# A feed-forward weight block in eight gets its low part by an adding DMA

## The chip, the cores and the metric

The kernel runs on one NeuronCore of one Trainium2 chip. The metric is the device time of one execution in microseconds. A core has a matrix engine (TensorE, PE in the profile, with its weight loads as PEld), VectorE (DVE), ScalarE (ACT), GpSimd (POOL), and SyncE (SP), which here only issues DMAs. DMAs run on 16 DMA engines; those issued by SP are "hardware dynamic", those issued by GpSimd "software dynamic".

## The reference

Two transformer blocks follow each other on 256 tokens of width 2048, in fp32. The first has differential attention, a gated recurrence, cross attention and a feed-forward; the second a pooling mixer, gated linear attention and a feed-forward. The change touches only the two feed-forwards:

```python
FFN_HIDDEN = ((8 * D_MODEL // 3 + 255) // 256) * 256      # 5632
h = rms_norm(x, ffn_pre_g[l])
gate, up = jnp.split(h @ w_ffn_in[l], 2, axis=-1)
x = x + rms_norm((jax.nn.silu(gate) * up) @ w_ffn_out[l], ffn_post_g[l])
...
f = (jax.nn.silu(h @ w_ffn_gate[l]) * (h @ w_ffn_up[l])) @ w_ffn_down[l]
x = x + rms_norm_2(f, norm_ffn_post[l])
```

## The kernel before

All weights come as one stream of 961 slots of 128 x 1024 fp32 (512 KB). Every matrix product is made from two parts of each operand in the format fp32r: a high part, which is the value copied into fp32r, and a low part, which is value less high part. Three products (high x high, high x low, low x high) make up for the short mantissa.

A slot passes through four buffers of each kind (NR = NH = 4):

- SP (`sync`, L2339) loads slot i into `RAW[i % 4]`. It may do so when the low part of slot i-4 has been made, since that is the last to read RAW.
- ScalarE (`scalar`, `upto`, L1054) copies RAW into `RH[i % 4]`, when the load has landed and slot i-4 has been multiplied.
- VectorE (`vector`, `upto`, L1554) writes `RL[i % 4] = RAW - RH`. Six slots in the program have this done by GpSimd instead (`on_pool`, L2173); none of them is in the set that the change takes.
- TensorE (`tensor`) waits for the high part by `s_hi` and for the low part in `wait_low`, multiplies, and counts `s_slot`.

Every engine has its instructions in a fixed order. The order of copies and side work is set by `through`: for each slot i of a group, `upto(i + LA)` with LA = 3 makes the parts up to slot i+3, then the side tasks of slot i follow, and at the last slot of a pass the eviction of its results.

A gate or up group has 8 slots, two passes of four. `by_feature` multiplies a slot as 8 matmuls with the high weights (each 512 columns, high and low activations together) and 8 with the low weights (256 columns). At even positions of a pass the high ones come first, at odd positions (`turned`) the low ones. So TensorE's rows show runs of 16 high and 16 low matmuls: a low run holds positions 0 and 1 or positions 2 and 3, a high run positions 1 and 2 or position 3 and the next pass's 0. Four pairs of PSUM banks serve the passes in turn.

At the end of a pass ScalarE copies the low sum out of PSUM (128x512, L1039). VectorE adds the high sum and multiplies by the row scale. At the end of a gate group ScalarE then takes silu (128x1024, AR<-AR); at the end of an up group VectorE multiplies by the gate and ScalarE writes the high part of the hidden activations (B_HL<-AR in the first feed-forward, A_HL<-AR in the second). Only after these does ScalarE go on to the high copy of slot last+4, which is position 3 of the next group's first pass. The copies for positions 0 to 2 have been made before.

The first feed-forward ("F") has groups Fg0, Fu0, Fg1, ... in three parts (0 to 3, 4 to 7, 8 to 10), each followed by four output groups (Fo0_0 ...). The second ("H") has the same order. The first slot of Fg0 is 176, that of Fg1 192, and every F group starts at a multiple of 8. That of Hg0 is 697, and every gate or up group of H starts at a multiple of 8 plus 1.

Of the kernel before, what the change touches and what calls it, by code (L numbers as in the profile page):

```python
# [7 lines left out]
F32 = mybir.dt.float32  # L8
# [3 lines left out]
ALU = mybir.AluOpType  # L12
# [16 lines left out]
NR, NH, LA = 4, 4, 3  # L29
# [123 lines left out]
def build(nc, A, out, scratch):  # L153
    ctx = ExitStack()
    with ctx:

        def sb(name, shape, dt=F32):
            return ctx.enter_context(nc.sbuf_tensor(name, shape, dt))

        def sem(name):  # L160
            return ctx.enter_context(nc.semaphore(name))

        RAW = sb("RAW", [P, NR, 1024])
        RH = sb("RH", [P, NH, 1024], F32R)
        RL = sb("RL", [P, NH, 1024], F32R)
# [17 lines left out]
        def U(k, n=1):  # L183
            return AR[:, k * 2048:(k + n) * 2048]
# [25 lines left out]
        slots, passes, unit, turns = [], {}, {}, [0]  # L210
# [23 lines left out]
        groups = {n: [i for ids in passes[n] for i in ids] for n in passes}  # L234

        def first(name):
            return groups[name][0]
# [4 lines left out]
        def low_rank_parts(i):  # L242

            return [R[:, i % NH, :].rearrange("p (k r n) -> p k r n", r=4, n=32) for R in (RH, RL)]

        def low_rank_raw(i):
            raw = RAW[:, i % NR, 0:256].rearrange("p (k n) -> p k n", n=16)
            return [raw[:, 8 * h:8 * h + 8, :].unsqueeze(2).broadcast_to([P, 8, 4, 16]) for h in range(2)]  # L250
# [10 lines left out]
        on_pool = {i for n in ("cq", "co0", "co1", "Fg0", "Hg0") for i in groups[n][1:2]} | {first("K0")}  # L261
        pool_before = [sum(j in on_pool for j in range(i)) for i in range(len(slots) + 1)]


        s_eye, s_gains, s_load, s_memld = sem("eye_loaded"), sem("gains_loaded"), sem("setup_loaded"), sem("mem_loaded")
        s_x, s_xt, s_table = [sem(f"x_loaded_{q}") for q in range(4)], [sem(f"x_turned_loaded_{c}") for c in range(5)], sem("table_wanted")
# [2 lines left out]
        s_raw = [sem(f"raw_loaded_{r}") for r in range(NR)]  # L269
        s_first_raw, s_first_hi = sem("first_half_slot_loaded"), sem("first_half_slot_high_made")  # L270
        s_hi, s_lo_v, s_lo_p = sem("high_made"), sem("low_made_by_vector"), sem("low_made_by_pool")
        s_slot, s_half = sem("slot_multiplied"), sem("first_half_multiplied")
        s_init = sem("pool_constants_set")
        s_low_sum = sem("low_sum_copied")
# [151 lines left out]
        for x in range(4):  # L426
            j, part = x // 2, x % 2
# [92 lines left out]
        def tensor(g):  # L520
# [7 lines left out]
            def wait_low(i):  # L528
                if i in on_pool:
                    g.wait_ge(s_lo_p, pool_before[i + 1])  # L530
                else:
                    g.wait_ge(s_lo_v, i + 1 - pool_before[i + 1])

            def wait_unit(name, p=0):
                if name in norm_of and p == 0:
# [498 lines left out]
        def scalar(g):  # L1034
# [3 lines left out]
            def act(o, i, f=ACT.Copy, scale=1.0, bias=0.0, accum=None):  # L1038
                return g.activation(o, i, f, bias=bias, scale=scale, accum_out=accum)  # L1039

            def upto(n):
                while made[0] <= min(n, len(slots) - 1):
                    i = made[0]
                    made[0] += 1
                    g.wait_ge(s_raw[i % NR], 16 * (i // NR + 1))
                    if i >= NH:
                        g.wait_ge(s_slot, i - NH + 1)
                    if i == first("LR"):
                        for both, raw in zip(low_rank_parts(i), low_rank_raw(i)):
                            t = act(both[:, :, :, 0:16], raw)  # L1050
                        t.then_inc(s_hi, 1)
                        continue
                    m = slots[i][1] * slots[i][2]
                    act(RH[:, i % NH, 0:m], RAW[:, i % NR, 0:m]).then_inc(s_hi, 1)  # L1054

            def through(name, evict=None, home=None, guard=(), early=None):

# [442 lines left out]
            for j in range(4):  # L1500

                for p, ids in enumerate(passes[f"yb{j}"]):
                    n = 2 * j + p
# [15 lines left out]
        def vector(g):  # L1519
# [3 lines left out]
            def tt(o, a, b, f):  # L1523
                return g.tensor_tensor(o, a, b, f)  # L1524
# [16 lines left out]
            def upto(n):  # L1541
                while made[0] <= min(n, len(slots) - 1):
                    i = made[0]
                    made[0] += 1
                    if i in on_pool:
                        continue
                    m, h = slots[i][1] * slots[i][2], i % NH
                    g.wait_ge(s_hi, i + 1)
                    if i == first("LR"):
                        for both, raw in zip(low_rank_parts(i), low_rank_raw(i)):  # L1550
                            t = tt(both[:, :, :, 16:32], raw, both[:, :, :, 0:16].bitcast(F32), ALU.subtract)
                        t.then_inc(s_lo_v, 1)
                        continue
                    tt(RL[:, h, 0:m], RAW[:, i % NR, 0:m], RH[:, h, 0:m].bitcast(F32), ALU.subtract).then_inc(s_lo_v, 1)  # L1554
# [603 lines left out]
        def gpsimd(g):  # L2158
# [3 lines left out]
            def upto(n):  # L2162
                while made[0] <= min(n, len(slots) - 1):
                    i = made[0]
                    made[0] += 1
                    if i not in on_pool:
                        continue
                    m, h = slots[i][1] * slots[i][2], i % NH
                    g.wait_ge(s_hi, i + 1)
                    if i == first("K0"):  # L2170

                        g.wait_ge(s_xv, 8 * 2 + 8)
                    g.tensor_tensor(RL[:, h, 0:m], RAW[:, i % NR, 0:m], RH[:, h, 0:m].bitcast(F32),  # L2173
                                    ALU.subtract).then_inc(s_lo_p, 1)
# [143 lines left out]
        def sync(g):  # L2318
            xv = A["x"][0].rearrange("(b p) d -> p b d", p=P)
            xt = A["x_turned"].rearrange("p (k t) -> p k t", t=T)  # L2320
            mv = A["mem"][0].rearrange("(b p) d -> p b d", p=P)
            mt = A["mem_turned"].rearrange("p (k t) -> p k t", t=T)
            ov = out[0].rearrange("(b p) d -> p b d", p=P)
            for i, (src, per, w) in enumerate(slots):
                if i < 4:

                    ks = slice(4 * i, 4 * i + (4 if i else 2))
                    g.dma_start(XT[:, ks, :], xt[:, ks, :]).then_inc(s_xt[i], 16)
                if i == 0:
                    g.dma_start(RAW[:, 0, 0:512], src[:, 0:512]).then_inc(s_first_raw, 16)  # L2330
                    g.dma_start(RAW[:, 0, 512:1024], src[:, 512:1024]).then_inc(s_raw[0], 16)
                    g.dma_start(XT[:, 2:4, :], xt[:, 2:4, :]).then_inc(s_xt[4], 16)
                    continue
                if i >= NR:
                    if i - NR in on_pool:
                        g.wait_ge(s_lo_p, pool_before[i - NR + 1])
                    else:
                        g.wait_ge(s_lo_v, i - NR + 1 - pool_before[i - NR + 1])
                g.dma_start(RAW[:, i % NR, 0:per * w], src).then_inc(s_raw[i % NR], 16)  # L2339
                if i in X_AT:  # L2340
                    q = X_AT.index(i)
                    half, b = X_HALF[q]
                    hs = slice(1024 * half, 1024 * half + 1024)
                    g.dma_start(X[:, b, hs], xv[:, b, hs]).then_inc(s_x[q], 16)
                if i == 10:
                    g.wait_ge(s_nlo, 8)
                    g.dma_start(setup[0:32, 0:384], A["c_hot"]).then_inc(s_load, 16)
                    g.dma_start(setup[0:8, 384:768], A["c_dead"]).then_inc(s_load, 16)
                    g.dma_start(setup[0:32, 768:776], A["rel_bias"]).then_inc(s_load, 16)
                    g.dma_start(setup[:, 776:1032], A["lambdas"].broadcast_to([P, 256])).then_inc(s_load, 16)  # L2350
                    g.dma_start(U(8)[:, 0:1024], A["c_mask"]).then_inc(s_load, 16)
                if i in (16, 18, 20, 22):
                    b, hs = (i - 16) // 4, slice(512 * (i % 4), 512 * (i % 4) + 1024)
                    g.dma_start(MEM[:, b, hs], mv[:, b, hs]).then_inc(s_memld, 16)
                if i in (30, 32, 34, 36):
                    c = (i - 30) // 2
                    g.wait_ge(s_mem_a, 2)
                    g.dma_start(MT[:, 4 * c:4 * c + 4, :], mt[:, 4 * c:4 * c + 4, :]).then_inc(s_mt[c], 16)
            for b in range(2):
                for c in range(4):  # L2360
                    cs = slice(512 * c, 512 * c + 512)
                    g.wait_ge(s_xv, 8 * 4 + 4 * b + c + 1)
                    g.dma_start(ov[:, b, cs], X[:, b, cs]).then_inc(s_out, 16)
            g.wait_ge(s_out, 8 * 16)
# [53 lines left out]
```

## Time and profile before

| | us |
|---|---|
| median of 3 runs | 2800.67 |
| lowest, highest | 2799.9, 2801.0 |
| span of the profiled execution | 2798.1 |
| its own time | not listed beside the profile; the median is 2.6 above the span |
| TensorE busy | 2776.8 (99%) |
| VectorE busy | 1762.7 (63%) |
| ScalarE busy | 1390.9 (50%) |
| GpSimd busy | 66.7 (2%) |
| mean granted clock of TensorE | 0.999 |

The span runs from the first to the last instruction. A row of the profile groups instructions by source line, engine and operation; nearly all matmuls, ScalarE operations and VectorE operations go through helpers and so share the lines 523, 1039 and 1524, and are told apart by the names of what they write and read. A group's idle time is what its engine stood still just before it, with the releaser that ended it.

### The profile page before, as it was taken

To read this page: it belongs to the slowest core of one execution; us is meant where nothing else is said; L and a number is where in the kernel's file an instruction comes from. 1 tells how busy PE (TensorE), PEld (TensorE's weight loads), DVE (VectorE), ACT (ScalarE), POOL (GpSimd) and SP (SyncE) were. 2 spreads that over 40 slices of the span, in tenths; PEclk is the share of its full clock that TensorE was granted. 3 is DMA by queue.
4 is the path that set the end of the run, shared out by engine and by line. 5 is a ranking of instruction groups with operands and counts; after the bars stand their busy time and mean duration, and the time that the engine had idled before them with its cause. 6 is when DMAs were issued, how large, how long until landed. Compare 5 with 4: busy or idle time off the path is not lost.

```text
span 2798.1 us, 39631 instructions
## 1 busy us (share of the span) xinstructions
PE 2776.8 (99%) x16396; PEld 2386.5 (85%) x16396; DVE 1762.7 (63%) x2003; ACT 1390.9 (50%) x1701; POOL 66.7 (2%) x55
## 2 busy tenths in 40 slices
PE   9999999999999999999999999999999999999998
PEld 7888888888888888888888888888888888888887
DVE  6778966565545655567778845666566545565566
ACT  5666544564444443445546545554454444443443
POOL 0000000000000000000011000000000000000000
PEclk9999999999999999999999999999999999999999
DMA  8555455565565566555555554565555555556555
GB/s 322 188 166 174 151 191 170 175 197 190 191 191 187 186 197 193 190 188 170 196 169 175 174 191 157 182 203 194 193 185 193 190 189 180 200 189 197 189 188 158
DMA packets 144437, 525.37 MB, mean 188 GB/s; under 512 B 16081, under 2 KB 16641, under 8 KB 143617
## 3 DMA queue, kind: packets, MB, share of 16 engines
q1 hardware_dynamic: 142528, 514.71, 55.8%
q0 software_dynamic: 1440, 7.88, 0.8%
q8 instruction: 129, 2.11, 0.3%
q14 instruction: 52, 0.42, 0.0%
q10 hardware_dynamic: 288, 0.24, 0.0%
HBM read 520.66 MB, written 2.11 MB: 187 GB/s over the span
## 4 chain that ended last, share of the span: by engine, by line
PE 97%; DVE 2%; issue 0%; ACT 0%; DMA 0%; POOL 0%; SPq 0%; DVEq 0%; POOLq 0%; ACTq 0%
PE PS L523 96%; DVE X L1530 1%; PE PS L526 0%; DVE AR L1524 0%; DVE RL L1524 0%; DVE A_HL L1530 0%; DMA AR<-in_x_turned 0%; ACT SP L1039 0%; POOL ST L2195 0%; ACT RH L1039 0%; DVE AR L1732 0%; DVE B_HL L1530 0%; DVE AR L1527 0%; ACT L1039 0%; DVE AR L1780 0%
## 5 line engine op out<-in xcount | busy, mean ns | idle before, releaser
L1524 DVE TENSOR_TENSOR RL<-RAW,RH 128x1024 fp32r<-128x1024 f32 x954 | 1156.9, 1225 | 774.9 <-ACT RH L1039 773.5
L1039 ACT ACTIVATE RH<-RAW 128x1024 fp32r<-128x1024 f32 (+1 forms) x962 | 1005.0, 1056 | 827.7 <-PE PS L523 810.7
L523 PE MATMUL PS<-A_HL,RH 128*128 128x512 f32 (+1 forms) x3280 | 790.0, 392 | 4.8 <-DVE A_HL L1530 4.8
L523 PEld LDWEIGHTS PS<-A_HL,RH 128*128 128x128 f32 (+1 forms) x3280 | 600.4, 188 | 124.3 <-issue 4.2
L523 PE MATMUL PS<-RH,A_HL 128*128 128x512 f32 x1728 | 538.2, 390 | 0.0
L523 PE MATMUL PS<-B_HL,RH 128*128 128x512 f32 x1856 | 444.4, 391 | 0.9 <-DVE B_HL L1530 0.9
L523 PEld LDWEIGHTS PS<-A_HL,RL 128*128 128x128 f32 (+1 forms) x3280 | 422.4, 191 | 18.9 <-DVE RL L1524 0.9
L523 PE MATMUL PS<-A_HL,RL 128*128 128x256 f32 (+1 forms) x3280 | 435.1, 285 | 0.0
L523 PEld LDWEIGHTS PS<-B_HL,RH 128*128 128x128 f32 x1856 | 340.9, 188 | 67.1 <-DVE B_HL L1530 1.2
L523 PEld LDWEIGHTS PS<-RH,A_HL 128*128 128x128 f32 x1728 | 324.4, 188 | 67.5 <-issue 0.2
L523 PE MATMUL PS<-RL,A_HL 128*128 128x512 f32 x864 | 336.2, 389 | 0.0
L1524 DVE TENSOR_TENSOR AR<-PS,AR 128x512 f32<-128x512 f32 (+2 forms) x232 | 160.1, 695 | 178.0 <-ACT AR L1039 166.6
L1039 ACT ACTIVATE AR<-PS 128x512 f32<-128x512 f32 (+1 forms) x185 | 113.4, 615 | 302.4 <-PE PS L523 300.2
L523 PE MATMUL PS<-RH,B_HL 128*128 128x512 f32 x832 | 257.7, 390 | 0.6 <-DVE B_HL L1524 0.6
L523 PEld LDWEIGHTS PS<-B_HL,RL 128*128 128x128 f32 x1856 | 238.0, 191 | 9.0
L523 PE MATMUL PS<-B_HL,RL 128*128 128x256 f32 x1856 | 241.9, 283 | 0.0
L523 PEld LDWEIGHTS PS<-RL,A_HL 128*128 128x128 f32 x864 | 162.2, 188 | 33.6 <-issue 0.2
L523 PEld LDWEIGHTS PS<-RH,B_HL 128*128 128x128 f32 x832 | 156.2, 188 | 33.4 <-issue 1.0
L523 PE MATMUL PS<-RL,B_HL 128*128 128x512 f32 x416 | 161.9, 389 | 0.0
L1524 DVE TENSOR_TENSOR AR<-AR 128x512 f32<-128x512 f32 (+3 forms) x187 | 139.8, 778 | 3.7
L1039 ACT ACTIVATE AR<-AR 128x1024 f32<-128x1024 f32 (+2 forms) x84 | 86.2, 1036 | 55.6 <-DVE AR L1524 52.0
L1524 DVE TENSOR_TENSOR AR<-AR,RR 128x512 f32<-128x512 f32 x139 | 95.9, 691 | 4.7
(113 smaller groups left out, 852.9 us busy)
## 6 DMA issues: line engine op xcount, KB each, us to landing
RAW<-in_stream SPq DMA_DIRECT2D x959, 512.0 KB, 4.2
X<-in_x SPq DMA_DIRECT2D x4, 512.0 KB, 7.0
AR<-in_mem SPq DMA_DIRECT2D x4, 512.0 KB, 6.8
AR<-in_mem_turned SPq DMA_DIRECT2D x4, 512.0 KB, 5.0
out_x<-X SPq DMA_DIRECT2D x8, 256.0 KB, 2.7
AR<-in_x_turned SPq DMA_DIRECT2D x3, 512.0 KB, 8.0
AR<-scratch POOLq DMA_DIRECT2D x1, 1024.0 KB, 8.1
AR<-in_mix_post_g POOLq DMA_DIRECT2D x1, 1024.0 KB, 8.4
```

The lines of the kernel that those rows point to most:

```text
L523: return g.matmul(o, l, r, start=start, stop=stop, skip_group_check=True)
L1039: return g.activation(o, i, f, bias=bias, scale=scale, accum_out=accum)
L1524: return g.tensor_tensor(o, a, b, f)
L1530: return g.scalar_tensor_tensor(o, a, s, b, f0, f1)
```

## The change

In gate and up groups other than Fg0 and Hg0, a slot whose number leaves 3 when divided by 8 gets its low part another way. ScalarE, after the high copy, writes the high part once more with scale -1 into RL. GpSimd waits for that and issues a DMA with `accum_op=ALU.add` from RAW into RL, which leaves RAW less the high part there. TensorE and SP wait for this DMA where they waited for VectorE. VectorE's count of low parts leaves these slots out.

```diff
+        on_dma = [i for n in groups if n[:2] in ("Fg", "Fu", "Hg", "Hu") for i in groups[n] if i % 8 == 3 and n not in ("Fg0", "Hg0")]
+        dma_before = [sum(j < i for j in on_dma) for i in range(len(slots) + 1)]
+
+        def by_vector_upto(i):
+            return i + 1 - pool_before[i + 1] - dma_before[i + 1]
...
+        s_neg, s_lo_d = sem("negative_high_made"), sem("low_made_by_dma")
...
             def wait_low(i):
                 if i in on_pool:
                     g.wait_ge(s_lo_p, pool_before[i + 1])
+                elif i in on_dma:
+                    g.wait_ge(s_lo_d, 16 * dma_before[i + 1])
                 else:
-                    g.wait_ge(s_lo_v, i + 1 - pool_before[i + 1])
+                    g.wait_ge(s_lo_v, by_vector_upto(i))
...
                     act(RH[:, i % NH, 0:m], RAW[:, i % NR, 0:m]).then_inc(s_hi, 1)
+                    if i in on_dma:
+                        act(RL[:, i % NH, 0:m], RAW[:, i % NR, 0:m], scale=-1.0).then_inc(s_neg, 1)
...
-                    if i in on_pool:
+                    if i in on_pool or i in on_dma:
                         continue
...
+                    if i in on_dma:
+                        g.wait_ge(s_neg, dma_before[i + 1])
+                        g.dma_start(RL[:, i % NH, :].bitcast(F32), RAW[:, i % NR, :], accum_op=ALU.add).then_inc(s_lo_d, 16)
                     if i not in on_pool:
                         continue
...
                     if i - NR in on_pool:
                         g.wait_ge(s_lo_p, pool_before[i - NR + 1])
+                    elif i - NR in on_dma:
+                        g.wait_ge(s_lo_d, 16 * dma_before[i - NR + 1])
                     else:
-                        g.wait_ge(s_lo_v, i - NR + 1 - pool_before[i - NR + 1])
+                        g.wait_ge(s_lo_v, by_vector_upto(i - NR))
```

## Rows read from the trace of the kernel before

**Rows 1.** The page: busy time of each engine, with its share.

```profile
PE 2776.8 (99%) x16396; PEld 2386.5 (85%) x16396; DVE 1762.7 (63%) x2003; ACT 1390.9 (50%) x1701; POOL 66.7 (2%) x55
```

**Rows 2.** The page: the chain that ended last, by engine.

```profile
PE 97%; DVE 2%; issue 0%; ACT 0%; DMA 0%; POOL 0%; SPq 0%; DVEq 0%; POOLq 0%; ACTq 0%
```

**Rows 3.** The waits of TensorE's weight loads: us in total, times, longest.

```profile
PEld PS L523 <- DVE RL L1524: 0.9, 2, 0.6
```

**Rows 4.** The page: costliest groups, with busy time and mean of one.

```profile
L1524 DVE TENSOR_TENSOR RL<-RAW,RH 128x1024 fp32r<-128x1024 f32 x954 | 1156.9, 1225 | 774.9 <-ACT RH L1039 773.5
L1039 ACT ACTIVATE RH<-RAW 128x1024 fp32r<-128x1024 f32 (+1 forms) x962 | 1005.0, 1056 | 827.7 <-PE PS L523 810.7
```

**Rows 5.** Timeline of ScalarE in F: start, length of the stretch.

```profile
637.45 1.99 ACT L1039 ACTIVATE RH<-RAW 128x1024 fp32r<-128x1024 f32 x2
...
660.09 1.06 ACT L1039 ACTIVATE B_HL<-AR 128x1024 fp32r<-128x1024 f32 x1 [2.88 <-DVE AR L1524]
661.05 2.94 ACT L1039 ACTIVATE RH<-RAW 128x1024 fp32r<-128x1024 f32 x3
```

**Rows 6.** Timeline of TensorE in F, the same stretch.

```profile
641.52 2.08 PE L523 MATMUL PS<-A_HL,RL 128*128 128x256 f32 x16
...
658.22 2.08 PE L523 MATMUL PS<-A_HL,RL 128*128 128x256 f32 x16
...
663.78 2.08 PE L523 MATMUL PS<-A_HL,RL 128*128 128x256 f32 x16
665.70 2.68 PE L523 MATMUL PS<-A_HL,RH 128*128 128x512 f32 x11
```

**Rows 7.** Timelines of ScalarE and TensorE in F, after an output group.

```profile
833.63 1.05 ACT L1039 ACTIVATE RH<-RAW 128x1024 fp32r<-128x1024 f32 x1
...
839.89 2.08 PE L523 MATMUL PS<-A_HL,RL 128*128 128x256 f32 x16
```

**Rows 8.** Timelines of ScalarE and TensorE in H.

```profile
2102.29 1.06 ACT L1039 ACTIVATE RH<-RAW 128x1024 fp32r<-128x1024 f32 x1 [1.71 <-PE PS L523]
2105.03 0.60 ACT L1039 ACTIVATE AR<-PS 128x512 f32<-128x512 f32 x1 [1.68 <-PE PS L523]
...
2113.42 1.06 ACT L1039 ACTIVATE RH<-RAW 128x1024 fp32r<-128x1024 f32 x1 [1.01 <-PE PS L523]
...
2112.21 2.08 PE L523 MATMUL PS<-B_HL,RL 128*128 128x256 f32 x16
```

**Rows 9.** DMA issues: engine, count, KB each, median us to landing.

```profile
RAW<-in_stream SPq DMA_DIRECT2D x959, 512.0 KB, 4.2
...
AR<-in_w_pool POOLq DMA_DIRECT2D x1, 1024.0 KB, 8.9
...
AR<-in_norm_ffn_post POOLq DMA_DIRECT2D x1, 1024.0 KB, 5.8
...
AR<-in_gate_up_rows POOLq DMA_DIRECT2D x1, 512.0 KB, 6.4
...
scratch<-AR POOLq DMA_DIRECT2D x1, 12.0 KB, 3.0
```

**Rows 10.** DMA queues: packets, MB, share of 16 engines' span.

```profile
q1 hardware_dynamic: 142528, 514.71, 55.8%
```

**Rows 11.** Timeline of SP's issues, 655 to 667 us.

```profile
656.21 0.33 SPq L2339 DMA_DIRECT2D RAW<-in_stream  x1
...
663.57 2.60 SPq L2339 DMA_DIRECT2D RAW<-in_stream  x3
```

**Rows 12.** Timeline of TensorE at the start, and stretches with clock.

```profile
9.42 1.84 PE L523 MATMUL PS<-A_HL,RH 128*128 128x512 f32 x4 [1.80 <-DVE A_HL L1530]
...
8.00:12.00 4.00, 2.58 (x9) 2.23 (x10) 3.61 (x8) 3.31 (x7) 0.00 (x0) 0.71 1.02 419
12.00:20.00 8.00, 8.00 (x44) 7.09 (x44) 8.00 (x13) 6.84 (x12) 0.00 (x0) 0.93 1.02 399
...
1296.00:1304.00 8.00, 5.57 (x38) 4.18 (x37) 6.83 (x13) 4.22 (x11) 2.50 (x2) 1.00 0.00 0
```

## The prediction

> **What bounds the kernel now.** I read the page's busy rows first: TensorE (PE) is busy 2776.8 of 2798.1 us, VectorE 63%, ScalarE 50%, GpSimd 2% [rows 1]. The reader is to see that relief of VectorE is worth something only where TensorE waits for it. The chain that ended last says the same: 97% of the span is TensorE [rows 2]. Then the waits of the weight-load row of TensorE: the waits for a low weight block (RL, from VectorE) come to 0.9 us in two places out of some 950 such blocks [rows 3]. So the whole gain that a faster low block can give is about 0.9 us, 0.03%. A difference of 0.2% (5.6 us) is about what a measurement of this kernel can tell from none. What is left to ask is whether the new, longer way of making a low block stays hidden.
>
> **What the change touches.** The slots with i % 8 == 3 in gate and up groups other than Fg0 and Hg0: 21 in the first feed-forward (F: ten gates, eleven ups) and 21 in the second (H). F groups begin at slots divisible by 8, so there the slot is position 3 of a pass of four, and by_feature takes its low half first (odd positions are turned). H groups begin one slot off (697, 705, ...), so there it is position 2, high half first.
>
> **Removed.** 42 VectorE subtractions of 1225 ns [rows 4], 51 us on an engine that has idle time. TensorE waited for it 0.9 us in all [rows 3]: worth 0.
>
> **Added on ScalarE.** 42 negated copies. Each has the form of the high copy, 1056 ns [rows 4], 44 us in all. Two such copies in a row take 1.99 us, three 2.94 [rows 5], so one more costs 0.94 us of delay to what ScalarE has queued: the high copies of the next slots, whose use lies behind the slot in question. ScalarE is half idle, so by itself this is hidden; its cost is that it stands ahead of the DMA in the new chain.
>
> **Added on GpSimd and the DMA engines.** The chain of a low block was: high copy, subtraction. It becomes: high copy, negated copy, GpSimd's wait, a software DMA of 512 KB that adds RAW onto RL, TensorE's wait. Ahead of these DMAs GpSimd's queue holds only small side work of the stage's start, and it is busy 2% of the span [rows 1], so its own queue adds nothing. I give the two hand-overs (ScalarE to GpSimd, DMA to TensorE) 0.1 us together, a guess too small to matter: 0.1 us more would be 2 us in the sum.
>
> How much time is there? I read the end of the high copy and the start of the low matmuls for each kind of place.
>
> - F, gate group after an up group (8 places: g1, g2, g3, g5, g6, g7, g9, g10). ScalarE must first write the hidden block (660.09), then makes three high copies from 661.05 on; the first is our slot. As two copies in a row take 1.99 us, the negated copy would end at 661.05 + 1.99 = 663.04 [rows 5]. The low run of 16 matmuls that starts at 663.78 and gives way to the next high run 1.91 us later holds positions 2 and 3, eight matmuls each [rows 6]; ours start at 663.78 + 0.96 = 664.74. Room for the DMA: 1.7, less 0.1: 1.6 us.
> - F, up group after a gate group (11 places). The high copies follow silu: 637.45, negated copy to 639.44 [rows 5]; low matmuls at 641.52 + 0.96 = 642.48 [rows 6]. Room 2.9 us.
> - F, gate group after an output group (g4, g8). 833.63 + 1.99 = 835.62, against 839.89 + 0.96 = 840.85 [rows 7]. Room 5.1 us.
> - H, 21 places. The high copy is made before the group's eviction: 2102.29, so the negated copy ends at 2104.28, and the next thing that ScalarE does starts at 2105.03, untouched. The low run is needed at 2112.21 [rows 8]. Room 7.8 us.
>
> What does the DMA take from issue to landing, L? No row shows an adding DMA between two SBUF tiles. Nearest rows [rows 9]: a 12 KB store from GpSimd 3.0 us (the fixed part); the only 512 KB load from GpSimd 6.4; 1 MB loads from GpSimd 5.8 to 8.9; 512 KB loads from SP 4.2 in the median. The main queue's 142528 packets took 55.8% of 16 engines' span: 175 ns for a mean of 3.6 KB, about 0.2 us for 4 KB [rows 10]. 128 rows over 16 engines are 8 packets each, 1.6 us. The added DMA moves bytes out of two tiles, so I count the transfer twice: 3.0 + 3.2 = 6.2. In F it has the engines nearly alone: the last stream load was issued at 656.21, and SP is then held by the very semaphore of our slot (before, until 663.57) [rows 11]. Lower bound of L: 3.0 + 1.6 = 4.6, an add that costs as a copy. Upper: four times the transfer, 3.0 + 6.4 = 9.4, close to the slowest POOL load, 8.9. I take 6.4, the row that is nearest in size and queue, and beside 6.2.
>
> The Trainium skill (DMA: Bandwidth & Descriptors, Anatomy of one DMA) fits a software DMA as 2.0 us plus its bytes over 436 GB/s; that would be 3.2 us here, an estimate by that page, and the stalls 16 us in all. This trace's rows on GpSimd's queue stand well above the fit (6.4 for 512 KB, 5.8 and more for 1 MB), so I keep it as a rival only.
>
> Nothing else can fill the gap: TensorE's queue is in order, so it stands still from the end of position 2 until L is over. **The sum at L = 6.4:** 8 x (6.4 - 1.6) + 11 x (6.4 - 2.9) + 2 x (6.4 - 5.1) = 38.4 + 38.5 + 2.6 = 79.5 us; H costs 0 with 1.4 us to spare. In general it is 19 L - 44.7 for L from 2.9 to 5.1, 21 L - 54.9 above 5.1, and 21 (L - 7.8) more above 7.8.
>
> **What is late next.** SP waits with load i+4 (and all behind it) until the DMA lands, in place of the subtraction. In F it lands when TensorE resumes; load i+4 takes 4.2 us, the high and low blocks 2.3 more, and TensorE wants them 4 slots on. Two slots take 5.56 us (663.78 less 658.22) [rows 6], so that is 11.1 us. The next loads are bunched behind it at 1.6 us each and are wanted 2.8 us apart. Each stall is made good before the next, 8 slots later; none adds to another. In H the load goes out at 2104.3 + 6.5 = 2110.8, lands at 2115, and the high copy slips by 1.7 us (it was at 2113.42 [rows 8]), of about 6 us of room. Nothing on TensorE.
>
> **The clock.** The granted clock is 1.00 nearly everywhere. It once fell: after TensorE had stood still for 1.80 us before 9.42, in a start where it had worked little, 8 to 12 us shows 0.71 and 12 to 20 shows 0.93, a mixture of the 2.4 and the 1.2 GHz level; the loss is 4 x 0.29 + 8 x 0.07 = 1.7 us. At 1296 to 1304, with 2.4 us idle in 8, it stayed 1.00 [rows 12]. The new stalls of 3.5 to 4.8 us are longer than any in this trace; I count a fall at half of the 19 long ones: 0.5 x 19 x 1.7 = 16 us, between 0 and 32.
>
> **Forecast.** 2798.1 + 79.5 + 16 = 2893.7 us of span. The median of the runs is 2.6 us above the span: 2896.
>
> **The rivals.**
>
> 1. Likeliest (0.53): F stalls, H is hidden, L between 5.1 and 7.8. Stalls of 52 to 109 us, with the clock 0 to 32 more: 2853 to 2942.
> 2. The adding DMA is slow, L over 7.8 (0.28). For it: no row shows what an addition costs on these engines, and TensorE is the bound in H as well, where 21 more places begin to pay. L = 9.4: 142 + 34 = 176, with all falls of the clock 208: 3009. Against: 9.4 is above every GpSimd load.
> 3. The addition costs no more than a copy, L from 3.9 to 5.1 (0.12). It runs inside SBUF, nearly alone. L = 4.6: 8 x 3.0 + 11 x 1.7 = 43 us, 2843 without falls of the clock. Against: the only 512 KB row of this queue has 6.4.
> 4. Nearly all of the transfer lies inside the 3.0 us that even 12 KB takes, so L is 2.3 to 3.9 (0.04). At 0.2 us over the 12 KB row, L = 3.2: 8 x 1.6 + 11 x 0.3 = 16 us, 2817. Against: every larger transfer of this queue takes 5.8 and more [rows 9]. This is the case that the fit of the Trainium skill named above describes.
> 5. The other side: not slower (0.03). The mechanism is that the DMA fits into the 1.6 us after an up group, or nearly: it decides at L = 2.3, where 8 x 0.7 = 5.6 us is 0.2%; the time would be 2801. Faster by over 0.2% is not to be had, with 0.9 us of waits to win.
>
> That the change doesn't do what it says (the DMA late only in name, TensorE finding its low block ready) is rival 5's price as well and has no row for it.
>
> **How the numbers follow.** The prediction is the likeliest case. The range takes in the bounds of L: 4.6 without the clock (2843, a little lower, 2838, for a shorter hand-over) to 9.4 with it (3009, 3012). Chances: faster 0.01, within 0.2% 0.03, slower 0.96.
>
> **What the profile after would show.** The new row to read is TensorE waiting for a DMA onto RL, some 21 times, 3 to 5 us each: about eight long, eleven shorter by 1.3 us, two short, none in H. If H has them, L is over 7.8. GpSimd issues 42 DMAs of 512 KB; their median landing is the term I am least sure of. VectorE's subtractions should count 912 in place of 954, ScalarE's copies 42 more. SP's waits should move to the DMA. The granted clock in the F stretch shows the second term. I am wrong if the landing is not within 5 to 8 us, or if the slots behind a stall stall again.

## The result, and the profile after

The changed kernel takes 2862.61 us (median of 4 runs, 2860.01 to 2864.96) against 2800.31 us before: 1.0224 times as long, 95% interval 1.0212 to 1.0237, 62 us more. The forecast was 2896, 96 us more, in a range of 2838 to 3012.

The page of the changed kernel first: busy times, and the chain that ended last. The matmul line is 530 now, ScalarE's 1048, VectorE's 1535.

```profile
span 2858.2 us, 39673 instructions
...
PE 2794.3 (98%) x16396; PEld 2397.7 (84%) x16396; DVE 1712.1 (60%) x1961; ACT 1429.8 (50%) x1743; POOL 103.1 (4%) x97
...
PE 91%; DMA 3%; DVE 3%; ACT 2%; issue 1%; POOL 0%; DVEq 0%; SPq 0%; POOLq 0%; ACTq 0%
...
L1535 DVE TENSOR_TENSOR RL<-RAW,RH 128x1024 fp32r<-128x1024 f32 x912 | 1105.5, 1225 | 774.2 <-ACT RH L1048 772.8
```

VectorE lost 51 us of work, as its row says, and nobody gained by it. The chain was 97% TensorE [rows 2]. Now DMA and ScalarE have entered it. The waits of the weight loads name the place:

```profile
PEld PS L530 <- DMA RL<-RAW: 46.6, 19, 3.2
PEld PS L530 <- issue: 22.5, 60, 2.4
...
PEld PS L530 <- DVE RL L1535: 0.2, 1, 0.2
```

The first row is new: 46.6 us in 19 waits, where before had 0.9 us for all low blocks [rows 3]. Asked for stretches of time, all 19 lie before 1330 us, in the first feed-forward, and none in the second. Then the adding DMA itself, from the list of DMA issues and from the answer on the tile RL (duration of the issue on GpSimd, and time to landing):

```profile
RL<-RAW POOLq DMA_DIRECT2D x42, 512.0 KB, 4.5
...
L2179 POOL DMA_DIRECT2D RL<-RAW x42: 852/862/938, 595.5 to 2761.9; - x42
...
DMA to landing us min/median/max: 4.5/4.5/5.0
...
q0 software_dynamic: 7488, 29.90, 4.8%
```

It lands after 4.5 us with hardly any spread. This is the number that no row of before showed. The timeline of one wait, a gate group after an up group, has the whole chain:

```profile
667.57 1.06 ACT L1048 ACTIVATE B_HL<-AR 128x1024 fp32r<-128x1024 f32 x1 [2.88 <-DVE AR L1535]
...
668.53 1.04 ACT L1048 ACTIVATE RH<-RAW 128x1024 fp32r<-128x1024 f32 x1
...
669.48 1.04 ACT L1048 ACTIVATE RL<-RAW 128x1024 fp32r<-128x1024 f32 x1
670.43 3.11 ACT L1048 ACTIVATE RH<-RAW 128x1024 fp32r<-128x1024 f32 x3
670.81 0.86 POOL L2179 DMA_DIRECT2D RL<-RAW  x1 [24.68 <-ACT RL L1048]
671.04 1.13 PEld L530 LDWEIGHTS PS<-A_HL,RL 128*128 128x128 f32 x8
671.27 1.11 PE L530 MATMUL PS<-A_HL,RL 128*128 128x256 f32 x8
...
675.39 1.78 PEld L530 LDWEIGHTS PS<-A_HL,RL 128*128 128x128 f32 x8 [3.22 <-DMA RL<-RAW]
675.39 2.08 PE L530 MATMUL PS<-A_HL,RL 128*128 128x256 f32 x8 [3.02 <-DMA RL<-RAW]
677.06 4.15 PEld L530 LDWEIGHTS PS<-A_HL,RH 128*128 128x128 f32 x16
677.27 4.37 PE L530 MATMUL PS<-A_HL,RH 128*128 128x512 f32 x16
```

Read it downwards. ScalarE writes the hidden block, then the high copy, then the negated copy, which ends at 670.52. GpSimd starts 0.29 us later, the DMA lands 4.5 us after that, and the weight load follows at 675.39. The low run of 16 matmuls of [rows 6] has been cut in two, with 3.0 us between the halves in which TensorE stood still (the weight load waited 3.2, as it runs 0.2 us ahead). There is a second thing: the eight low matmuls after the wait took 2.08 us, where the eight before it took 1.11, and the 16 high ones 4.37, where a run takes 3.82 at full clock. The clock had fallen. Stretches of the changed kernel (length, busy times of the engines, then granted clock, DMA share and GB/s):

```profile
655.00:675.00 20.00, 17.38 (x102) 15.23 (x100) 12.21 (x12) 9.69 (x10) 0.86 (x1) 1.00 0.55 166
675.00:680.00 5.00, 4.61 (x18) 4.10 (x19) 0.00 (x0) 0.14 (x1) 0.00 (x0) 0.66 0.69 241
680.00:700.00 20.00, 19.29 (x112) 16.87 (x110) 9.94 (x10) 10.65 (x12) 0.85 (x1) 1.00 0.55 174
...
580.00:760.00 180.00, 164.14 (x922) 143.97 (x922) 89.29 (x90) 83.50 (x92) 7.69 (x8) 0.98 0.60 190
...
850.00:1060.00 210.00, 194.22 (x1062) 169.11 (x1061) 99.85 (x98) 92.60 (x99) 6.90 (x8) 0.97 0.58 186
...
1150.00:1330.00 180.00, 168.93 (x897) 145.97 (x896) 92.40 (x90) 81.24 (x91) 4.31 (x5) 0.98 0.60 191
```

One fall costs 5 x 0.34 = 1.7 us, the figure of [rows 12]. The three gate and up stretches of F lose 180 x 0.02 + 210 x 0.03 + 180 x 0.02 = 13.5 us of full clock. The clock column is rounded to 0.01, so this is good to about 3 us. The timeline gives it more closely. From the end of a wait to the next run of 16 low matmuls TensorE takes 4.7 us at full clock. After seven of the eight long waits it took 1.4, 1.4, 2.9, 1.6, 1.6, 1.6 and 1.6 us more, 12 us in all; after the eighth and after all eleven short waits it took no longer than 4.7. Waits of 46.6 and clock losses of 12 to 13.5 us are 59 to 60 us, and the spans differ by 2858.2 - 2798.1 = 60.1. One or two microseconds at most are left to explain in the size; the causes were put to the test.

### The profile page after: what moved, and what is told of

It reads as the page before. It is cut to its first block, busy times and chain, and to the rows that moved or that the text cites. A ratio compares the mean times of both kernels' runs of the same rounds, so it can differ in the third digit from the quotient of the medians.

```text
span 2858.2 us, 39673 instructions
## 1 busy us (share of the span) xinstructions
PE 2794.3 (98%) x16396; PEld 2397.7 (84%) x16396; DVE 1712.1 (60%) x1961; ACT 1429.8 (50%) x1743; POOL 103.1 (4%) x97
## 4 chain that ended last, share of the span: by engine, by line
PE 91%; DMA 3%; DVE 3%; ACT 2%; issue 1%; POOL 0%; DVEq 0%; SPq 0%; POOLq 0%; ACTq 0%
PE PS L530 90%; DMA RL<-RAW 3%; DVE AR L1535 1%; ACT RH L1048 1%; ACT RL L1048 1%; DVE X L1541 1%; PE PS L533 0%; DVE RL L1535 0%; DVE A_HL L1541 0%; ACT AR L1048 0%; DMA RAW<-in_stream 0%; ACT SP L1048 0%; POOL ST L2209 0%; DVE AR L1743 0%; DVE B_HL L1541 0%
## 5 line engine op out<-in xcount | busy, mean ns | idle before, releaser
L1535 DVE TENSOR_TENSOR RL<-RAW,RH 128x1024 fp32r<-128x1024 f32 x912 | 1105.5, 1225 | 774.2 <-ACT RH L1048 772.8
L530 PE MATMUL PS<-A_HL,RH 128*128 128x512 f32 (+1 forms) x3280 | 799.4, 396 | 4.4 <-DVE A_HL L1541 4.4
L530 PEld LDWEIGHTS PS<-A_HL,RH 128*128 128x128 f32 (+1 forms) x3280 | 607.4, 191 | 126.8 <-issue 4.4
L530 PE MATMUL PS<-A_HL,RL 128*128 128x256 f32 (+1 forms) x3280 | 442.8, 286 | 42.7 <-DMA RL<-RAW 42.7
L530 PEld LDWEIGHTS PS<-A_HL,RL 128*128 128x128 f32 (+1 forms) x3280 | 426.0, 192 | 65.2 <-DMA RL<-RAW 46.6
```

Source lines behind the costliest of these rows:

```text
L530: return g.matmul(o, l, r, start=start, stop=stop, skip_group_check=True)
```

## The experiments

Each was timed beside the kernel before. All ratios below are to it. The waits (of the weight loads) and the clock are those of the profiled execution.

| | us | ratio, 95% interval | waits on the DMA | granted clock |
|---|---|---|---|---|
| h_only | 2799.58 | 1.0000 (0.9991 to 1.0010) | none | 0.999 |
| pos2 | 2800.11 | 1.0003 (0.9994 to 1.0012) | none | 0.999 |
| pos3 | 2924.68 | 1.0445 (1.0428 to 1.0463) | 95.4 us, 39 | 0.988 |
| high_first | 2812.83 | 1.0048 (1.0033 to 1.0063) | 15.8 us, 19 | 0.999 |
| early_copy | 2800.04 | 1.0002 (0.9992 to 1.0011) | none | 0.999 |
| no_negative | 2831.11 | 1.0113 (1.0098 to 1.0128) | 28.6 us, 19 | 0.998 |
| plain_copy | 2815.35 | 1.0057 (1.0042 to 1.0072) | 14.9 us, 19 | 0.999 |
| half_width | 2829.53 | 1.0106 (1.0089 to 1.0123) | 22.9 us, 19 | 0.996 |
| filler | 2852.39 | 1.0188 (1.0173 to 1.0203) | 4.4 us, 9 | 0.999 |
| half_of_all | 2904.40 | 1.0374 (1.0339 to 1.0410) | 108.2 us, 74 | 0.995 |
| five_raw | 2885.15 | 1.0313 (1.0296 to 1.0330) | 83.9 us, 66 | 0.996 |
| quarter_of_all | 2802.30 | 1.0009 (1.0000 to 1.0019) | 0.2 us, 1 | 0.997 |

### Where the slot sits

**h_only**: the second feed-forward alone.

```diff
-on_dma = [i for n in groups if n[:2] in ("Fg", "Fu", "Hg", "Hu") for i in groups[n] if i % 8 == 3 and ...]
+on_dma = [i for n in groups if n[:2] in ("Hg", "Hu") for i in groups[n] if i % 8 == 3 and ...]
```

> The adding DMAs are made only in the second feed-forward (21 of the 42), which takes its slot at position 2 of a pass. Theory (the place decides: there the room of 7.8 us hides a landing of 4.5): no TensorE wait on the DMA, the time of before, 2800 us, within 0.2%. Rival (the extra DMA traffic and ScalarE copies cost wherever they are): half of the 62 us, 2831.

No waits and no time. 21 of the 42 DMAs cost nothing, so the load that they and the negated copies put on the engines is not the cause there; pos2 asks the same of the first feed-forward.

**pos2** and **pos3**: the same position of the first pass in both feed-forwards.

```diff
+on_dma = [groups[n][2] for n in groups if n[:2] in ("Fg", "Fu", "Hg", "Hu") and n not in ("Fg0", "Hg0")]
```

> All 42 blocks are at position 2 of the first pass of their group, in both feed-forwards. Theory (place): the F waits vanish too, 2800 us within 0.2%, clock falls only where before has them. Rival (something of the first feed-forward other than the position): still 40 to 62 us slower, 2840 to 2862.

> All 42 at position 3, where the low half comes first. Theory (place): the second feed-forward pays what the first does, 19 waits more with 46 us and some 7 clock falls with 12 us: 2862 + 60 = 2922 us. Rival (the second feed-forward hides it for another reason): 2862.

(pos3 has `groups[n][3]`.) pos2 has all 42 DMAs, 21 of them in F, and takes the time of before. The time went from 2800 to 2925 by this one index, 2922 expected. 20 of its 39 waits are in the second feed-forward. The weight loads of pos3, and the addition in it:

```profile
PEld PS L530 <- DMA RL<-RAW: 95.4, 39, 3.5
...
DMA to landing us min/median/max: 4.5/4.5/6.0
```

**high_first**: still position 3, but the high half before the low.

```diff
-turned = (i - ids[0]) % 2 == 1 and i > 3
+turned = (i - ids[0]) % 2 == 1 and i > 3 and i not in on_dma
```

> As the changed kernel, but on the slots of the adding DMA TensorE takes the high half first, so that 8 high matmuls (1.75 us) lie before the wait. Theory (waits of 3.2 and 1.9 us, and the clock falls because of them): 8 x 1.45 + 11 x 0.15 = 13 us of waits, no clock falls, 2814 us. Rival (the clock falls have another cause and stay): 2829.

The time is 2813 us, 2814 expected; the rival's 2829 is out. Eight high matmuls stand before the wait and cover 1.6 us of it ((46.6 - 15.8) / 19 by the waits of the weight loads), and the clock doesn't fall. In TensorE's timeline the wait after an up group is 1.2 us long and the run after it has its ordinary length, eight high ones in 2.00 us and the next 16 low ones in 2.08:

```profile
668.66 1.22 PE L530 MATMUL PS<-A_HL,RL 128*128 128x256 f32 x8 [1.19 <-DMA RL<-RAW]
669.72 2.00 PE L530 MATMUL PS<-A_HL,RH 128*128 128x512 f32 x8
671.56 2.08 PE L530 MATMUL PS<-A_HL,RL 128*128 128x256 f32 x16
```

**early_copy**: position 3 and low half first, as in the changed kernel, but ScalarE makes both copies before silu or the hidden block.

```diff
+                        if i == ids[-1] and i + LA + 1 in on_dma:
+                            upto(i + LA + 1)
                         if evict and i == last(name):
                             evict(unit[name, 0])
```

> As the changed kernel, position 3 and low half first in F as there, but at a group's end ScalarE makes the high copy and the negated copy of that slot before silu or the hidden block, not after. The negated copy is then ready at about 659.1 on the scale of the trace of before, the DMA lands 0.3 + 4.5 later, 663.9, wanted at 664.74. Theory (what sits ahead in ScalarE's queue takes the room away, not the position as such): no waits, 2800 us within 0.2%. Rival (low half first alone is too early): waits stay near 2 and 1 us, 2820 to 2830.

ScalarE's and GpSimd's timelines:

```profile
656.65 1.05 ACT L1048 ACTIVATE RH<-RAW 128x1024 fp32r<-128x1024 f32 x1
657.60 1.05 ACT L1048 ACTIVATE RL<-RAW 128x1024 fp32r<-128x1024 f32 x1
659.64 1.06 ACT L1048 ACTIVATE B_HL<-AR 128x1024 fp32r<-128x1024 f32 x1 [0.99 <-DVE AR L1537]
...
658.94 0.85 POOL L2181 DMA_DIRECT2D RL<-RAW  x1 [21.41 <-ACT RL L1048]
```

The time is that of before. The copies fill time in which ScalarE had stood still for VectorE, 2.88 us of it before [rows 5]. The hidden block is no later. The DMA, issued at 658.94, lands at 663.4, before the low half is wanted at 663.34 + 0.96 = 664.3. So neither the position nor the order of halves is at fault by itself, but what stands ahead in ScalarE's queue.

### What the chain is made of

**no_negative**

```diff
-                    if i in on_dma:
-                        act(RL[:, i % NH, 0:m], RAW[:, i % NR, 0:m], scale=-1.0).then_inc(s_neg, 1)
...
-                        g.wait_ge(s_neg, dma_before[i + 1])
+                        g.wait_ge(s_hi, i + 1)
```

> ScalarE's negated copy is left out, and GpSimd issues the DMA when the high copy is ready, so the low block is RAW plus what the buffer held. Theory (the copy stands in the chain with 0.95 us): waits of 2.25 and 0.95 us, 8 x 2.25 + 11 x 0.95 = 28 us, fewer clock falls (0 to 5 of them, 1.7 us each): 2829 to 2838. Rival (its time is hidden behind something on GpSimd): 2862.

The waits fell from 46.6 to 28.6 us, 18.0 by 19 waits: 0.95 us each. The time, 2831 us, is in the range expected. The negated copy lies in the chain with its whole length.

**plain_copy** and **half_width**

```diff
-g.dma_start(RL[:, i % NH, :].bitcast(F32), RAW[:, i % NR, :], accum_op=ALU.add)
+g.dma_start(RL[:, i % NH, :].bitcast(F32), RAW[:, i % NR, :])                          # plain_copy
+g.dma_start(RL[:, i % NH, 0:512].bitcast(F32), RAW[:, i % NR, 0:512], accum_op=ALU.add) # half_width
```

> The DMA copies RAW into RL in place of adding. Theory (the addition costs latency because bytes move out of two tiles): landing falls by about half of the transfer, from 4.5 to 3.1 us, waits of 1.8 and 0.5 us, 20 us, 2820. Rival (an addition lands as soon as a copy): landing 4.5, waits as before, 2862.

> The DMA adds only the first 512 of 1024 columns; the rest of the low block stays the negated high part. Splits the landing into a fixed part and a transfer. If the fixed part is 1.8 and the transfer 2.7 us: landing 3.15, waits of 1.85 and 0.55, 21 us, 2821. If the fixed part is 3.0 (the 12 KB row) and the transfer 1.6: landing 3.7, waits of 2.4 and 1.1, 31 us, 2831 to 2840.

The rows of the plain copy: landing, issue, and the software queue's share.

```profile
RL<-RAW POOLq DMA_DIRECT2D x42, 512.0 KB, 2.9
...
L2179 POOL DMA_DIRECT2D RL<-RAW x42: 527/527/577, 594.4 to 2717.2; - x42
...
q0 software_dynamic: 7488, 29.90, 2.7%
```

And of the addition on half the columns:

```profile
RL<-RAW POOLq DMA_DIRECT2D x42, 256.0 KB, 3.3
```

An addition lands after 4.5 us, a copy of the same size after 2.9; the rival of plain_copy, that both land alike, is out. Half the size takes 1.2 us off, so an addition of 512 KB is 2.1 fixed and 2.4 of transfer, if the transfer goes with the bytes. This is an estimate from two sizes with the same 128 rows, and no third size tests it. Of the 1.6 between copy and addition 0.33 can be the longer issue on GpSimd (0.86 against 0.53), since the landing is counted from the start of the issue. The other 1.2 to 1.3 would be transfer, that is, twice that of a copy; no copy of half the size was run. The queue rows say the same of the engines: over before's 0.8%, 42 additions took 0.048 x 2858.2 - 0.008 x 2798.1 = 115 us of each engine, 2.7 apiece, and 42 copies 0.027 x 2813.5 - 22 = 54 us, 1.3 apiece. By its landing (3.3) and its waits (22.9 us) half_width is near its first case (3.15 and 21 us, 2821). But its span is 30.2 us longer than before's, 7 more than its waits, and that case had counted no falls of the clock: three of them account for 4.7 of the 7 us (1.6 each in the timeline). Two lines of its timeline show a fall after a standstill of only 1.77 us, the 16 high matmuls taking 5.41 us in place of 3.82:

```profile
898.15 1.22 PE L530 MATMUL PS<-A_HL,RL 128*128 128x256 f32 x8 [1.77 <-DMA RL<-RAW]
899.21 5.41 PE L530 MATMUL PS<-A_HL,RH 128*128 128x512 f32 x16
```

So the length of a standstill alone doesn't decide. In the profiled executions the clock fell after seven of eight standstills of 3.0 us (the changed kernel), after one of eight of 2.1 us (no_negative), after three of eight of 1.8 us (half_width) and after none of eleven of 1.7 us (the changed kernel). What else decides stays open.

**filler**: useless matmuls in place of the waits.

```diff
+                        if i in on_dma and turned and name not in ("Fg4", "Fg8"):
+                            g.wait_ge(s_hi, i + 1)
+                            for e in range(14 if name[1] == "g" else 9):
+                                mm(PS[:, banks[e % 2], :], hi[:, e % 4, 0:P],
+                                   HL[:, k + e % 4, :, :].rearrange("p h t -> p (h t)"), False, False)
```

> As the changed kernel, but in 19 of the 21 F slots TensorE does 14 (gate) or 9 (up) high matmuls of the slot over again before it waits for the low half, adding wrong products. They fill the waits of 3.2 and 1.9 us. Theory (the standstill makes the clock fall): no clock falls but before's own, 46 us for the waits alone, 2847 us. Rival (the falls don't hang on the standstill): 2862.

In the timeline 14 fillers take 3.20 us and nine take 2.06 (0.229 each), so all are 8 x 3.20 + 11 x 2.06 = 48 us. TensorE still stands still for 1.9 us in two places, and its weight loads wait 4.4 us in nine. That is 50 to 53 us, and this span is 51.7 us longer than before's. TensorE is kept from its own work as long as in the changed kernel or a little longer, yet the kernel is 10 us faster than that one, and the clock stays up in the same three stretches:

```profile
580.00:760.00 180.00, 179.36 (x1007) 156.64 (x1006) 89.48 (x90) 84.26 (x93) 7.68 (x8) 1.00 0.61 193
850.00:1060.00 210.00, 210.00 (x1165) 183.25 (x1164) 104.81 (x102) 96.17 (x103) 6.88 (x8) 1.00 0.60 191
1150.00:1330.00 180.00, 178.70 (x945) 153.91 (x944) 92.12 (x88) 81.26 (x91) 4.30 (x5) 1.00 0.60 190
```

The standstill brings the clock down, not the DMA. The 2852 measured are 5 above the theory's 2847, by fillers a little longer than the waits and by the waits that were left; the rival's 2862 is out.

### How far the cover reaches

**half_of_all**, **five_raw** and **quarter_of_all** take even positions only, and a DMA semaphore for each RAW buffer (`s_lo_d[i % NR]`).

```diff
+on_dma = [i for n in groups if n[:2] in (...) for i in groups[n][::2] if n not in ("Fg0", "Hg0")]   # half_of_all
+NR, NH, LA = 5, 4, 3                                                                              # five_raw, besides
+on_dma = [i for n in groups if n[:2] in (...) for i in groups[n][2::4] if n not in ("Fg0", "Hg0")]  # quarter_of_all
```

(The lines for the semaphores are left out here.)

> Positions 0 and 2 of both passes, 168 adding DMAs in place of 42, with a semaphore for each buffer. How far does the cover of pos2 reach? Theory 1 (room of 7.8 us stays, engines have space): no TensorE waits, 2800. Theory 2 (an adding packet of 4 KB holds its DMA engine about 0.34 us, 2.7 us a block, a load 1.6 us; two loads and one addition are 5.9 us against TensorE's 5.56 us for two slots): the DMA engines become the bound of the gate and up groups, 336 slots, 168 x 0.35 = 59 us at most, 2820 to 2860.

> As half_of_all (2904 us), with five RAW buffers in place of four. Theory 1 (a buffer's round trip binds: load 4.3, high copy 1.05, negated copy 0.95, hand-over 0.3, addition 5.1, in all 11.7 us against 11.1 us for four slots): with five buffers a trip may take 13.9 us, the waits go, 2800 to 2815. Theory 2 (the DMA engines bind, share 0.94 in the gate and up stretches): only the rest up to a share of 1.0 is to be had, some 6% of about 1000 us of these stretches, 2840 or more.

> Position 2 of both passes, 84 additions, four RAW buffers, a semaphore for each buffer. Share of the DMA engines about 0.8 in gate and up stretches, and each passes its buffer with the room of 7.8 us, with ordinary slots between. Both theories of half_of_all: no or few waits, 2800 to 2806. If a bufferful of late loads adds up already at one slot in four: 2820 and more.

half_of_all is 105 us slower, more than either theory said. Its ScalarE waits and one stretch:

```profile
ACT RH L1049 <- PE PS L531: 529.8, 373, 3.8
ACT RH L1049 <- DMA RAW<-in_stream: 390.2, 148, 6.9
...
600.00:757.00 157.00, 147.14 (x829) 126.15 (x828) 58.26 (x60) 89.61 (x97) 21.56 (x25) 1.00 0.94 264
```

Loads come late, 390 us of waits on ScalarE where [rows 4] had TensorE as the releaser. Five buffers take these waits away:

```profile
ACT RH L1049 <- PE PS L531: 781.0, 525, 6.3
ACT RH L1049 <- DMA RAW<-in_stream: 47.7, 46, 3.0
...
600.00:757.00 157.00, 146.35 (x828) 125.76 (x827) 57.52 (x59) 89.75 (x95) 21.36 (x25) 1.00 0.96 263
```

But only 19 of the 105 us come back; theory 1 of five_raw, that all would, is out. The DMA engines' share is at 0.96 in this stretch (0.95 and 0.90 in two others), and an addition now lands after 6.4 us in the median, against 5.1 with four buffers. Two loads of 1.6 us and an addition of 2.7 are 5.9 us of every engine in the 5.56 us that TensorE needs for two slots; over 168 pairs that is an estimate of 57 us, of the 85 measured. This fits DMA engines that bind, with four buffers adding to it, but it is argued and not shown: no run took engine time off the additions at this rate, and the other 28 us stay open, but for some 9 us that the lower clock can account for (0.996 against 0.999). With one slot in four, the share in this stretch is 0.74:

```profile
600.00:757.00 157.00, 157.00 (x888) 138.08 (x887) 81.08 (x80) 84.12 (x91) 11.14 (x13) 1.00 0.74 232
```

TensorE is busy throughout, and the time is within 0.1% of before, as expected.

## Why the prediction was right, and where it was off

**The bound.** Right: VectorE's 51 us were worth nothing. No version here beats the kernel before, since its waits for low blocks are 0.9 us [rows 3]; the best are level with it.

**The places.** Right: 19 waits of DMA onto RL in F, none in H, in two sizes that differ by 1.3 us (3.2 and 1.9, waits of the weight loads). The forecast had 21; the two places after an output group had room enough for 4.5 us, and so they have no wait. h_only, pos2, pos3 and early_copy bear out that the room decides. The rooms had been read from [rows 5 to 8].

**The landing.** This is the term that was mis-sized: 6.4 us taken, 4.5 measured, so 19 L - 44.7 gives 41 us where 79.5 were forecast. By the prediction's own sign ("wrong if the landing is not within 5 to 8 us") this term was wrong. The case is its third rival by the landing (3.9 to 5.1), which had 0.12, and not the likeliest one. The measured waits, 46.6 us, lie below the 52 us at which the likeliest case begins; that the time still falls into its 2853 to 2942 is luck, since the losses of the clock made up for it. The third rival's reason was not the true one either: by the estimates above an addition costs twice a copy's transfer (2.4 against 1.2). What was too high was the fixed part, 2.1 us against the 3.0 of a 12 KB store to HBM [rows 9], and each of the two transfers, 1.2 against 1.6 for a load from HBM beside others. The nearest row in size and queue, 6.4, had been a load from HBM too. It has 7.9 in the changed kernel's trace, and 1 MB loads from 5.8 to 9.2: that row is no measure of a transfer inside SBUF with the engines nearly idle.

The fit that the Trainium skill gives (DMA: Bandwidth & Descriptors, Anatomy of one DMA), 2.0 us and the bytes over 436 GB/s, was set aside on the strength of those rows. For the plain copy it makes 3.2 us, an estimate by that page, and 2.9 was measured. For the addition the same 3.2 (rival 4) is too low, 4.5 was measured; with the bytes of both tiles counted, a step that is mine and not the page's, the estimate is 4.4. The traces agree with the fit to 0.3 us for these transfers inside SBUF, and not for the 512 KB load from HBM (6.4 and 7.9).

**The hand-overs.** 0.1 us was guessed. GpSimd starts 0.29 us after the negated copy and the weight load follows the landing by about 0.08: 0.37 together. That is 0.27 x 19 = 5 us more, so 41 becomes 46, and 46.6 were measured.

**The clock.** 1.7 us for a fall was right. The forecast took a fall at half of 19 waits, 16 us; there were seven falls and 12 us by the timeline (13.5 by the clock column), and filler and high_first show that the standstill brings them. They don't follow the waits evenly, as half of 19 supposed: seven came after the eight long waits and none after the eleven short ones. With standstills of 1.2 us and less in high_first there were none.

**The rivals.** A slow addition was out by the landing. So was "not slower", whose price at its own edge (a landing of 2.3 us) is 2806 by the sum, not the 2801 written there. Two errors had opposite signs, the landing (38 us too much) and the hand-overs (5 too little). The range held because it had been drawn down to a landing of 4.6 without falls of the clock.

**What is late next.** Right: SP's and ScalarE's later work caught up before the next stall, and no slot behind a stall stalled again. In the second feed-forward the high copy that was to slip by 1.7 us kept its place (2113.52 in h_only, 2113.42 before), as the landing was shorter. half_of_all shows where that ends.

## What to carry to other kernels

Before work moves from an idle engine to a longer chain, read for each place how long it is from the first input to the wanted output, and what stands ahead in the queue of the first engine: here two lines that put two copies ahead of silu or the hidden block were worth 62 us. A row of a transfer from HBM under load tells little of one inside SBUF; take fixed part and transfer apart. Most standstills of TensorE of about 3 us cost half as much again here through the clock (1.7 us). So it pays to put useful matmuls in front of a wait: eight of them took off not only 1.6 us of each wait but also the falls.

## What the runs showed of the hardware that was not expected

An adding DMA of 512 KB between two SBUF tiles lands after 4.5 us in the median and 5.0 at the most in the changed kernel, a copying one after 2.9. By the shares of the queue it holds each of the 16 engines for 2.7 us against 1.3, and its issue takes GpSimd 0.86 us against 0.53. GpSimd starts 0.29 to 0.30 us after the ScalarE instruction that it waits for, in all seven places of the first stretch of F. After a standstill of 3.2 us the granted clock was 0.66 over 5 us, that is, the lower level (1.2 GHz) for part of them; in the changed kernel this came after most, not all, of the eight long waits: after the first of them (3.04 us at 625.65) the next 16 high matmuls took their ordinary time:

```profile
625.65 1.22 PE L530 MATMUL PS<-A_HL,RL 128*128 128x256 f32 x8 [3.04 <-DMA RL<-RAW]
626.71 3.82 PE L530 MATMUL PS<-A_HL,RH 128*128 128x512 f32 x16
```
